# Two low-weight matmuls moved ahead of the last two high-weight matmuls in every full block of columns

## The reference

```python
def swiglu(h, w_gate, w_up, w_down):
    return (jax.nn.silu(h @ w_gate) * (h @ w_up)) @ w_down

for l in range(DEPTH):                       # DEPTH = 2
    x = x + 0.5 * swiglu(rms_norm(x, ffn1_norm[l]), ...)        # 1024 -> 2816 -> 1024
    z = rms_norm(x, mix_norm[l]) @ w_in[l]                      # 1024 -> 2816
    x = x + concat([diff_attention(z), conformer_conv(z), short_conv(z)]) @ w_out[l]
    hq = rms_norm(x, xa_norm[l]) @ xa_wq[l]
    kv = rms_norm(mem, mem_norm[l]) @ xa_wkv[l]                 # 256 memory tokens
    x = x + cross_attention(hq, kv) @ xa_wo[l]
    x = x + 0.5 * swiglu(rms_norm(x, ffn2_norm[l]), ...)
return rms_norm(x, final_norm)
```

## Time and profile before

| | before |
|---|---|
| time of 3 runs, us | 1144.94 median (1144.91 to 1145.62) |
| time of the profiled execution, us | 1145.19 |
| its span from first to last instruction, us | 1143.5 |
| mean granted TensorE clock | 0.998 of full speed |
| TensorE matmuls busy | 1135.6 us, 99% of the span, 6180 instructions |
| weight loads (beside the matmuls) | 982.3 us, 86% |
| VectorE busy | 857.4 us, 75% |
| ScalarE busy | 655.8 us, 57% |

### The profile page before, as it was taken

How to read it: one execution, slowest core, us unless ns; L and a number is a source line. 1 busy time by engine, 2 the same in 40 slices (tenths; PEclk the granted TensorE clock), 3 DMA queues, 4 the chain that set the end, 5 groups by cost and what they waited for, 6 DMA issues and landing times.

```text
span 1143.5 us, 15684 instructions
## 1 busy us (share of the span) xinstructions
PE 1135.6 (99%) x6180; PEld 982.3 (86%) x6180; DVE 857.4 (75%) x1164; ACT 655.8 (57%) x941; POOL 21.6 (2%) x63
## 2 busy tenths in 40 slices
PE   9999999999999999999999999999999999999997
PEld 8888888888889888888888888888888888888886
DVE  7877676899967686766777676669998676866765
ACT  6655556547755565554565555464577556745454
POOL 1000000000000000000000000000000000000000
PEclk9999999999999999999999999999999999999999
DMA  7856653644444366555547645544545444656561
GB/s 267 315 210 192 213 188 144 221 148 172 166 167 159 112 216 229 162 197 195 190 143 258 219 162 201 192 165 167 185 148 206 162 148 129 203 191 214 181 199 44
DMA packets 66265, 210.92 MB, mean 184 GB/s; under 512 B 5008, under 2 KB 24208, under 8 KB 61072
## 3 DMA queue, kind: packets, MB, share of 16 engines
q1 hardware_dynamic: 65216, 209.26, 53.3%
q10 hardware_dynamic: 976, 0.66, 0.2%
HBM read 208.85 MB, written 1.05 MB: 184 GB/s over the span
## 4 chain that ended last, share of the span: by engine, by line
PE 95%; DVE 4%; DVEq 1%; DMA 0%; issue 0%; ACT 0%; ACTq 0%
PE G L1693 28%; PE G L1705 14%; PE D L1545 10%; PE D L1543 10%; PE D L1544 10%; PE G L1638 3%; PE D L1638 3%; PE G L1543 3%; PE G L1545 3%; PE G L1544 3%; PE G L1647 2%; DVE w_lo L984 1%; PE D L1647 1%; DVE acc L1193 1%; PE D L1610 1%; DVEq L1195 1%
## 5 line engine op out<-in xcount | busy, mean ns | idle before, releaser
L984 DVE TENSOR_TENSOR w_lo<-w_raw,w_hi 128x2048 fp32r<-128x2048 f32 (+3 forms) x260 | 452.7, 1747 | 60.1 <-ACT w_hi L566 59.0
L566 ACT ACTIVATE w_hi<-w_raw 128x2048 fp32r<-128x2048 f32 (+3 forms) x260 | 380.9, 1474 | 35.7 <-PE D L1545 17.0
L1693 PE MATMUL G<-a,w_hi 128*128 128x512 f32 x1406 | 339.3, 391 | 0.0
L1693 PEld LDWEIGHTS G<-a,w_hi 128*128 128x128 f32 x1406 | 258.9, 188 | 51.3 <-issue 0.9
L1089 DVE TENSOR_TENSOR zqk<-G,zqk 128x512 f32<-128x512 f32 x88 | 60.8, 691 | 125.2 <-ACT zqk L645 124.5
L1705 PEld LDWEIGHTS G<-kx_lo,w_lo 128*128 128x128 f32 x1152 | 139.6, 188 | 2.8
L1705 PE MATMUL G<-kx_lo,w_lo 128*128 128x256 f32 x1152 | 140.3, 279 | 0.0
L1543 PE MATMUL D<-w_hi,hT_hi 128*128 128x512 f32 x352 | 137.3, 390 | 0.0
L1545 PE MATMUL D<-w_hi,hT_lo 128*128 128x512 f32 x352 | 137.1, 389 | 0.0
L1544 PE MATMUL D<-w_lo,hT_hi 128*128 128x512 f32 x352 | 137.0, 389 | 0.0
L645 ACT ACTIVATE zqk<-G 128x512 f32<-128x512 f32 x88 | 52.2, 593 | 137.9 <-PE G L1705 137.8
(11 more groups left out here) (264 smaller groups left out, 1357.8 us busy)
## 6 DMA issues: line engine op xcount, KB each, us to landing
w_raw<-w_dram SPq DMA_DIRECT2D x120, 1024.0 KB, 5.0
w_raw<-w_dram SPq DMA_DIRECT2D x143, 512.0 KB, 5.1
m_raw<-memT_dram SPq DMA_DIRECT2D x2, 1024.0 KB, 9.7
w_raw<-w_dram SPq DMA_DIRECT2D x6, 256.0 KB, 6.2
w_raw<-w_dram SPq DMA_DIRECT2D x8, 128.0 KB, 4.0
vx<-mem_dram SPq DMA_DIRECT2D x1, 1024.0 KB, 10.9
x<-x_dram SPq DMA_DIRECT2D x2, 256.0 KB, 5.5
gbc<-fin_dram SPq DMA_DIRECT2D x1, 512.0 KB, 6.8
```

What stands on the lines that cost most here:

```text
L566: A(w_hi[:, part(i)], w_raw[:, part(i)], ACT.Copy).then_inc(s_hi, 1)
L984: V.tensor_tensor(w_lo[:, part(i)], w_raw[:, part(i)], w_hi[:, part(i)].bitcast(F32), ALU.subtract).then_inc(s_lo, 1)
L1693: last = M(banks[b], whi[:, at:at + P], both, start=k == 0 and not low_first, stop=k == KD - 1 and low_first, skip_group_check=low_first)
```

## The change

In `gate_up` and `head_columns`, a block that covers all 8 channel blocks, has H first and nothing put between is now multiplied in four pieces: H of channel blocks 0 to 6 (14 matmuls), L of channel block 0 (2), H of channel block 7 (2), L of channel blocks 1 to 7 (14). Blocks with `low_first`, with a `between`, or with fewer than 8 channel blocks are as before. In the second hunk of the diff, `gate_up`'s; the first does the same in `head_columns`, where it also fixes the offset into the block to the whole block's first k (`first`).

```diff
             def head_columns(src, whi, wlo, tiles, banks, ks, width, ready=None, between=None, low_first=False):
 
-                def high_weights():
+                def high_weights(ks=ks, first=ks[0]):
...
-                            at = (k - ks[0]) * width + d * P
+                            at = (k - first) * width + d * P
...
                 if low_first:
                     low_weights()
                     return high_weights()
+                if len(ks) == KD and between is None:
+                    high_weights(ks[:-1])
+                    low_weights(ks[:1])
+                    high_weights(ks[-1:])
+                    return low_weights(ks[1:])
                 high_weights()
...
                 if low_first:
                     low_weights()
                     last = high_weights()
+                elif len(ks) == KD:
+                    high_weights(ks[:-1])
+                    low_weights(ks[:1])
+                    high_weights(ks[-1:])
+                    last = low_weights(ks[1:])
                 else:
                     high_weights()
                     last = low_weights()
```

More of the change, by code:

```diff
@@ L1640, in high_weights, with low_weights @@
                     return last
-                def low_weights():
+                def low_weights(ks=ks, first=ks[0]):
                     for k in ks:
                         for d in tiles:
-                            at = (k - ks[0]) * width + d * P
+                            at = (k - first) * width + d * P
                             last = M(banks[d][:, T:], wlo[:, at:at + P], src[:, k, 0, :], start=k == 0 and low_first,
@@ L1683, in gate_up, with high_weights @@
                 banks = G[2 * (c % 2):2 * (c % 2) + 2]
-                def high_weights():
+                def high_weights(ks=ks):
                     for k in ks:
@@ L1698, in gate_up, with low_weights @@
                     pe.wait_ge(s_twin, 2 * l + f + 1)
-                def low_weights():
+                def low_weights(ks=ks):
                     for k in ks:
```

## The result

The changed kernel is slower: 1147.13 us median (1146.56 to 1148.97, 19 runs) against 1145.13 us (1144.72 to 1146.78, 19 runs) of the kernel before, measured beside it. The ratio is 1.0017 with a 95% interval of 1.001 to 1.0024: 2.0 us, three times the 0.6 that I forecast. The time lies 0.2 us over the top of my range (1144.2 to 1146.9).

A forecast was written before the change was run, and what follows sets the result against it. TensorE's matmuls bound the kernel, filling 99% of the span, so only intervals between their starts could change. 49 x (0.016 - 0.003) = 0.6 us on the median 1144.94 gave 1145.5 us, range 1144.2 to 1146.9.

The forecast's parts named there:

- The two H: H of channel block 7 behind the two moved L: together 0.47 us against 0.454, so +0.016.
- The 30 L: Long run of L behind the two H in a chunk pair: should take 3.50 us.
- Only two H follow it now, so only the first two intervals of the settling are paid: Added change from L to H in each of 49 blocks: costs +0.016 us.
- should take 3.66 as before: Last 16 H of a chunk pair, behind the 30 L: claimed unchanged at 3.66 us.
- the 0.013 forecast: Net cost per split block: 0.016 for L to H less 0.003 for H to L.
- upper end of 0.03 + 0.01 a block: Slow end over 49 blocks: whole settling 0.03, H to L change 0.01; 2.0 us slower.
- Neither sign that I named for being wrong: In the trace after: the long L run's pace moves over 0.002 us, or a wait stands between the pieces.
- The row that I used for L behind an unsettled group: Program start: 4 L behind 4 H take 0.47 us, 0.1175 each, against 0.1197 in long runs out of `a`.
- the width of 0.01: H to L change out of the second copy, without a row: costs at most the rounding, 0.01 us.
- The bound of 0.03 for a whole settling: L to H change, from above: 0.03 us if the H break the settling off and the L behind pay the rest.
- free: Rival for the split blocks: the two H's lost intervals come back; 1144.9 us, down to 1143.5; chance 0.30.
- The second copy's pace is lost: Rival: 30 L behind the pair fall back to 0.1197 us each in 36 blocks; 3.4 us, 1148.9; chance 0.04.

The follow-up runs named there:

- e4_one_copy_split: Kernel before with every L reading `a`, none the second copy, and `gate_up` alone split as in the change: 1148.42 us against 1145.10, ratio 1.0033.
- e3_one_copy_before: Kernel before in its own order, with every L reading `a` and none the second copy (still made): 1148.85 us against 1145.10, ratio 1.0033.

## Why the prediction was wrong

**Right.** That TensorE's intervals are all that can change, that no wait appears (1.3 us of them, had 1.5) and that the clock stays. The two H: 0.47 forecast, 0.466 measured. The 30 L: 3.50 and 3.50. The sign, and that the pace of the long run holds.

**Wrong: the step "Only two H follow it now, so only the first two intervals of the settling are paid".** This is true of the two H, and I let the account end there. I wrote that the last 16 H "should take 3.66 as before"; they take 3.69. Of the 0.054 us that a pair loses, 0.037 stand in these 16, and the two H (0.013) and the L (0.003) make the rest, against the 0.013 forecast. 36 x 0.037 = 1.3 us is what the forecast of 0.6 lacks of the 1.9. The settling of those 16 H was a term that I put at no change, with no row for a run of L entered in this way. My upper end of 0.03 + 0.01 a block was meant for a settling broken off and paid later, once; paid later it came dearer than if it had run its course: eleven intervals and 61 ns instead of five and 24. That the rise of 2.0 us equals my upper end, 49 x 0.04, is chance: 36 blocks paid 0.054 each and 13 paid nothing. Neither sign that I named for being wrong came, since the pace of the long run held and no wait appeared; what gave it away was the last 16 H.

**Wrong in the bound, and it could have been seen.** The row that I used for L behind an unsettled group was out of `a`, and out of `a` the unsettled state dies within eight L (`e4_one_copy_split`). There was no such row for the second copy. I took one operand's row for the other's, although showed that the two differ, and gave the missing case the width of 0.01. The bound of 0.03 for a whole settling was too low as well, and the trace of the kernel before could tell it. Two short matmuls of another kind stand ahead of the 16 H that begin chunk 2 there, and these 16 take 588.50 - 584.79 = 3.71 us:

```profile
584.55 0.28 PE L1774 MATMUL D<-hT_hi,mean_r 128*128 128x256 f32 x1
584.67 0.28 PE L1775 MATMUL D<-hT_lo,mean_r 128*128 128x256 f32 x1
584.79 3.87 PE L1693 MATMUL G<-a,w_hi 128*128 128x512 f32 x16
588.50 0.76 PE L1705 MATMUL G<-a,w_lo 128*128 128x256 f32 x5
```

The first interval, 271 ns, holds 0.044 us of the excess. The nine behind it are 229 233 235 225 230 236 229 232 232 and hold another 0.04: to 1 ns the intervals that close the long settling of the changed kernel. In the stretch of the earlier trace rows the same kind of group settles in five. So a settling of ten intervals was there before the change, and behind short groups it was not always of one length.

**The noise.** I put what a measurement can tell at 0.2%, 2.3 us. With 19 runs of each kernel the interval reaches 0.07%, 0.8 us, either way, and the 2.0 us stand clear of it.

**The 13 blocks out of `a`.** I charged them 0.013 each. They cost nothing: 11.107 against 11.113 a pair (`e4_one_copy_split` and `e3_one_copy_before`), and 0.03 us less over the ten blocks of `head_columns`. The 12 to 16 ns of the two H come back in the L behind. This is the mechanism of my rival "free", but in these blocks only.

**The rivals.** "The second copy's pace is lost" had the right suspicion, that what the run of L does hangs on how it is entered, and looked for it in the wrong place: the mean pace of the run doesn't move by a nanosecond, and the bill comes at its exit. The formula of the Trainium skill, "TensorE: Matmul & The Clock Gate", section "Back-to-back issue gap", knows the columns alone, and as I used it gave a cost of nothing; the section itself calls it the gap of an isolated matmul. The measurement says 1.9 us, and that the order and the place of an operand both count.

**Open.** What inside TensorE holds this state is not settled. The runs show that a state is there, that it repeats (36 pairs alike to a nanosecond or two), what sets it going (two or four H between runs of L, where six don't; or L in turn out of both tiles), what keeps it (L out of the second copy) and what ends it (six to eight L out of `a`, or three to eleven H). They don't show what about the second copy's place does this. It has another address, and its channel blocks follow one another where those of `a` have a low part between them; neither was varied by itself. Nor do they show whether the moving operand's side or the weights' side holds the state: in the pairs of the earlier trace rows and of the changed kernel nearly every weight load starts 2 to 4 ns behind a matmul's start, so the two keep step.

## What to carry to other kernels

In a kernel that TensorE bounds, cost a reordering over everything up to the next point where the intervals are back at their resting value, not only over the moved instructions: here two thirds of the price stood in matmuls that hadn't moved. Keep runs of matmuls of one length long; if a short piece must stand between two others, look at the intervals behind it one by one, since a group's total or mean hides a repeating pattern. Letting the piece settle (six H here, 0.027 us a pair) halved the cost; ending the run behind it on a cheap place (0.014) cost less still, but that place was found only by trying run lengths. And take the price of a case from a row with the same operands in the same places.

## What the runs showed of the hardware

Behind narrower matmuls (256 columns), matmuls of 512 columns start 230, 236, 229, 232 and 231 ns apart before they rest at 227, where the narrower run had itself settled. The pace of narrow matmuls with a new weight load each is 117 or 120 ns depending on which of two tiles with the same contents the moving operand lies in, and nearly the mean of both if they alternate (32 in 3.73, 3.83 and 3.79 us). Entered after only two or four wide ones, narrow matmuls out of one of the tiles don't come to rest in runs of up to 30 but go round 120, 113, 116, 118 ns, and the wide ones behind them then settle over 3, 8 or 11 intervals by the place at which the round is broken off: behind two wide ones, run lengths of 24, 26, 28 and 30 make the next 16 take 3.65, 3.69, 3.65 and 3.69 us, and 30 behind four make them take 3.67.
